# A paged attention cache's rope rows turned by VectorE during the projection, kept in DRAM, and read back as keys

## What is computed

```python
def step(carry, pages):                  # one page of 128 rows per sequence
    m, l, acc = carry
    ck = cache_ckv[pages]                # (8, 128, 256) latent rows
    kr = cache_krope[pages]              # (8, 128, 64)  rotary key rows
    s = mla_scores(q_lat, q_rope, ck, kr)    # q_lat.ck + q_rope.kr, scaled
    m_new = jnp.maximum(m, jnp.max(s, axis=-1))
    alpha = jnp.exp(m - m_new)
    p = jnp.exp(s - m_new[..., None])
    l = l * alpha + jnp.sum(p, axis=-1)
    acc = acc * alpha[..., None] + jnp.einsum('bhqk,bkc->bhqc', p, ck)
    return (m_new, l, acc), None
(m, l, acc), _ = lax.scan(step, (m0, l0, acc0), page_table.T)
```

## Time and profile before

| what | value |
|---|---|
| median of three runs | 2065.1 us (2063.27 to 2066.8) |
| the profiled execution's own time | 2068.19 us |
| its span, first to last instruction | 2066.4 us |
| TensorE busy | 1892.8 us (92%) |
| VectorE, ScalarE, GpSimd busy | 594.6, 443.1, 274.8 us |
| mean granted TensorE clock | 0.953 of full speed |
| moved by DMA | 400.28 MB, mean 194 GB/s |

### The profile page before, as it was taken

How to read it: one execution, slowest core, us unless ns; L and a number is a source line. 1 busy time by engine, 2 the same in 40 slices (tenths; PEclk the granted TensorE clock), 3 DMA queues, 4 the chain that set the end, 5 groups by cost and what they waited for, 6 DMA issues and landing times. The chain is left out here.

```text
span 2066.4 us, 27202 instructions
## 1 busy us (share of the span) xinstructions
PE 1892.8 (92%) x10878; PEld 1122.3 (54%) x10878; DVE 594.6 (29%) x1362; ACT 443.1 (21%) x934; POOL 274.8 (13%) x420
## 2 busy tenths in 40 slices
PE   7999999999999999988999997999498888988884
PEld 5644444444445656755666664565365555555551
DVE  3110000000003334334555555566412211111116
ACT  3211111100013333222444443222111101111103
POOL 1021111000000000002222220122411211111100
PEclk9999999999999999998999998999699899999997
DMA  8212220222110000005777775435589999999986
GB/s 250 82 72 73 78 73 31 78 78 78 58 53 1 1 1 1 1 0 224 286 269 280 274 271 217 178 131 181 197 347 420 420 418 412 418 403 402 409 334 253
DMA packets 91425, 400.28 MB, mean 194 GB/s; under 512 B 22656, under 2 KB 28256, under 8 KB 60544
## 3 DMA queue, kind: packets, MB, share of 16 engines
q1 hardware_dynamic: 71040, 297.50, 36.9%
q0 software_dynamic: 20160, 101.24, 13.0%
q10 hardware_dynamic: 128, 0.20, 0.0%
HBM read 372.44 MB, written 46.88 MB: 203 GB/s over the span
## 5 line engine op out<-in xcount | busy, mean ns | idle before, releaser
L795 PE MATMUL psum<-arena 128*128 128x512 f32 (+1 forms) x1280 | 526.1, 566 | 0.0
L795 PEld LDWEIGHTS psum<-arena 128*128 128x128 f32 x1280 | 238.9, 189 | 259.2 <-issue 234.7
L1224 PE MATMUL psum<-arena 128*64 128x256 f32 (+1 forms) x2048 | 286.4, 414 | 66.2 <-DMA arena<-in_w_up_dram 65.7
L1224 PEld LDWEIGHTS psum<-arena 128*64 128x64 f32 (+1 forms) x2048 | 204.8, 156 | 137.9 <-issue 82.2
L1839 DVE COPY arena<-psum 128x512 f32<-128x512 f32 (+5 forms) x52 | 27.8, 545 | 522.2 <-PE psum L863 226.4
L1007 PEld LDWEIGHTS psum<-arena 128*128 128x128 f32 x1280 | 142.2, 142 | 29.3 <-issue 26.0
L1007 PE MATMUL psum<-arena 128*128 128x128 f32 x1280 | 153.8, 276 | 2.4 <-DVEq L1887 2.4
L1243 PE MATMUL psum<-arena 128*64 128x512 f32 (+1 forms) x512 | 131.3, 595 | 0.7 <-DVE arena L2153 0.7
L1393 ACT ACTIVATE arena<-psum 128x512 f32<-128x512 f32 (+1 forms) x72 | 40.5, 562 | 411.8 <-PE psum L795 401.0
L1410 ACT COPY arena<-psum 128x512 f32<-128x512 f32 x160 | 90.5, 587 | 176.5 <-PE psum L1007 176.5
L1895 DVE COPY arena<-psum 128x512 f32<-128x512 f32 x160 | 109.8, 692 | 36.3 <-PE psum L1007 33.7
(11 more groups left out here) (304 smaller groups left out, 1941.2 us busy)
## 6 DMA issues: line engine op xcount, KB each, us to landing
arena<-in_w_gate_dram SPq DMA_DIRECT2D x64, 1024.0 KB, 12.0
arena<-in_w_up_dram SPq DMA_DIRECT2D x64, 1024.0 KB, 20.6
arena<-in_w_down_dram SPq DMA_DIRECT2D x64, 1024.0 KB, 22.0
arena<-in_w_in_dram SPq DMA_DIRECT2D x8, 2048.0 KB, 7.9
z_act<-arena SPq DMA_DIRECT2D x64, 256.0 KB
arena<-z_act SPq DMA_DIRECT2D x8, 2048.0 KB, 10.4
arena<-in_x_prompt_dram SPq DMA_DIRECT2D x16, 512.0 KB, 4.8
arena<-y_rows SPq DMA_DIRECT2D x8, 1024.0 KB, 9.9
```

The costliest lines, as they stand in the source:

```text
L795: last = mm(out[:, 0:w], xn_t[:, k, t * P:t * P + P], w_blk[n % 2][:, k, 0:w], start=(k == 0), stop=(k == KD - 1))
L1224: last = mm(bank(2 + u)[rows, DE * x:DE * x + DE], xg_t[u][:, k, rows], w_e[slot][x][:, k, :], start=(k == 0), stop=(k == KD - 1))
```

## The change

The rope rows leave stage 3's gather and its transposes.

In stage 1, once the early units are done, GpSimd gathers the `kr` rows of all 32 chunks one after the other into two raw buffers, VectorE turns each in two instructions of 32x32 blocks (128 x 512 each) into two turned buffers, and SyncE stores them with two transfers a chunk to a new DRAM scratch `rope_t` of 64 features by 2048 keys a chunk (16.8 MB in all). The stores stand in SyncE's list behind the z stores of tiles 42 to 57, two chunks a tile. GpSimd reaches its barrier only when all are stored.

In stage 3 SyncE loads one chunk's turned rows, 64 partitions of 8 KB, into one of four places (two tiles, upper or lower 64 partitions), from three scores ahead. A chunk is now eight units on four banks, and the rope round of `score` reads its keys from that place in pieces of 32 columns, all four products on the same half of the partitions. The other edits are bookkeeping: key rows of a unit are consecutive, one semaphore carries two former ones, and the counts of waits follow.

```diff
+FIRST_ROPE = 42
...
+        pre = [attn_base + 5 * D]
+        kr_raw = [take(PG * DR, pre).rearrange("p (r n) -> p r n", r=PG) for _ in range(2)]
+        kr_b = [take(PG * DR, pre).rearrange("p (c m) -> p c m", c=2) for _ in range(2)]
+        rope_t = nc.dram_tensor("rope_turned", [NCH * DR, PG * P], F32, kind="Internal").ap()
...
-        kr = [take(PG * DR, o).rearrange("p (r n) -> p r n", r=PG) for _ in range(4)]
+        kr_t2 = [take(PG * P, o) for _ in range(2)]
-        kr_tt = take(2 * 512, o).rearrange("p (g n) -> p g n", g=2)
...
-        turn_units = [("c", 0, 0), ("c", 0, 1), ("r", 0, 0), ("c", 1, 0), ("c", 1, 1),
-                      ("c", 2, 0), ("c", 2, 1), ("r", 1, 0), ("c", 3, 0), ("c", 3, 1)]
+        turn_units = [(j, c) for j in range(4) for c in range(2)]
...
+        def rope_home(n):
+            return kr_t2[n % 4 // 2][DR * (n % 2):DR * (n % 2) + DR, :]
+        PRE = NCH // 2
...
+            def rope_store(n):
+                sp.wait_ge(rk_t, n + 1)
+                for c in range(2):
+                    rows = DR * n + 32 * c
+                    sp.dma_start(rope_t[rows:rows + 32, :].rearrange("f (a m) -> a f m", a=4),
+                                 kr_b[n % 2][:, c, :]).then_inc(rk_mv[n % 2], 16)
...
+                    for n in range(2):
+                        if FIRST_ROPE <= b * NT + t < FIRST_ROPE + NCH // 2:
+                            rope_store(2 * (b * NT + t - FIRST_ROPE) + n)
...
+            def rope_load(n):
+                if n >= 4:
+                    sp.wait_ge(c_s, n - 3)
+                sp.wait_ge(rk_mv[n % 2], 32 * PRE + 16 * (n // 2))
+                sp.dma_start(rope_home(n), rope_t[DR * n:DR * n + DR, :]).then_inc(rk_mv[n % 2], 16)
...
             sp.wait_ge(ends, 8)
+            for n in range(2):
+                rope_load(n)
...
+            for n in range(2, NCH):
+                rope_load(n)
...
-                    if u >= 5:
-                        pe.wait_ge(kt_in[(u - 5) % 2], 5 * n + (u - 5) // 2 + 1)
+                    if u >= 4:
+                        pe.wait_ge(kt_in[u % 2], 4 * n + (u - 4) // 2 + 1)
...
+                rope = rope_home(q).rearrange("p (a r k) -> p r a k", a=4, r=PG)
...
-                                  ck_t[:, c, j, :] if c < 2 else kr_tt[half, j // 2, :], start=(c == 0), stop=(c == 2))
+                                  ck_t[:, c, j, :] if c < 2 else rope[:, 4 * j:4 * j + 4], start=(c == 0), stop=(c == 2))
...
-                        turned(n + 1, (6, 8))
+                        turned(n + 1, (6,))
...
+            for n in range(NCH):
+                if n >= 2:
+                    pool.wait_ge(rk_t, n - 1)
+                off = bass.IndirectOffsetOnAxis(ap=page_int[:, n:n + 1].bitcast(U32), axis=0)
+                pool.indirect_dma_start(kr_raw[n % 2].rearrange("p r c -> p (r c)"), None, kr_g, off).then_inc(c_in[n % 2], 16)
+            for u in range(2):
+                pool.wait_ge(rk_mv[u], 32 * PRE)
             stage_end(pool, 1)
...
-                pool.indirect_dma_start(kr[q].rearrange("p r c -> p (r c)"), None, kr_g, off).then_inc(c_in[q], 16)
...
+            for n in range(NCH):
+                dve.wait_ge(c_in[n % 2], 16 * (n // 2 + 1))
+                if n >= 2:
+                    dve.wait_ge(rk_mv[n % 2], 32 * (n // 2))
+                for c in range(2):
+                    last = V.transpose(kr_b[n % 2][:, c, :].rearrange("p (r k) -> p r k", r=PG),
+                                       kr_raw[n % 2][:, :, 32 * c:32 * c + 32])
+                last.then_inc(rk_t, 1)
             stage_end(dve, 1)
```

More of the change, by code:

```diff
@@ L440, in build @@
         z_stored = [sem(f"z_stored{i}") for i in range(2)]
-        lat_stored = sem("latent_stored")
+        rows_stored = sem("cache_rows_stored")
         lat_ready = sem("latent_ready")
@@ L456, in build @@
         c_tr = sem("cache_turned")
+        rk_t, rk_mv = sem("rope_blocks_turned"), [sem(f"rope_rows_moved{i}") for i in range(2)]
         kt_in = [sem("turned_by_act"), sem("turned_by_dve")]
@@ L506, in build @@
         block = ctx.enter_context(nc.Block())
[L510 to L511 removed]
+        turn_units = [(j, c) for j in range(4) for c in range(2)]
         NU = len(turn_units)
         def key_row(j, kk):
[L516 removed]
+            return 4 * j + kk
         def turned_at(u):
[L519 to L520 removed]
+            j, c = turn_units[u]
+            return ck_t[:, c, j, :]
+        def rope_home(n):
+            return kr_t2[n % 4 // 2][DR * (n % 2):DR * (n % 2) + DR, :]
+        PRE = NCH // 2
         def group_moves(what, n, out):
@@ L691, in _ @@
             sp.wait_ge(y_mm, NT)
-            sp.wait_ge(v_st, 16)
+            sp.wait_ge(rows_stored, 80)
             w_load(3, 3)
@@ L996, in turn, with score @@
                 for u in us:
-                    if u >= 5:
-                        pe.wait_ge(kt_in[(u - 5) % 2], 5 * n + (u - 5) // 2 + 1)
+                    if u >= 4:
+                        pe.wait_ge(kt_in[u % 2], 4 * n + (u - 4) // 2 + 1)
                     elif not first:
-                        pe.wait_ge(kt_in[(u + 5) % 2], 5 * n - 5 + (u + 5) // 2 + 1)
-                    kind, j, c = turn_units[u]
+                        pe.wait_ge(kt_in[u % 2], 4 * n - 4 + (u + 4) // 2 + 1)
+                    j, c = turn_units[u]
                     for kk in range(4):
[L1003 to L1007, removed]
+                        last = tr(bank(u % 4)[:, P * kk:P * kk + P], ck[q][:, key_row(j, kk), P * c:P * c + P], ident)
                     last.then_inc(c_tr, 1)
-            def score(n):
+            def score(n, q, loads):
+                half = slice(DR * (q % 2), DR * (q % 2) + DR)
+                rope = rope_home(q).rearrange("p (a r k) -> p r a k", a=4, r=PG)
                 for e in range(2):
-                    pe.wait_ge(kt_in[e], 5 * n + 5)
+                    pe.wait_ge(kt_in[e], 4 * n + 4)
+                pe.wait_ge(rk_mv[q % 2], 32 * PRE + 16 * loads)
                 for c in range(3):
                     for j in range(4):
-                        half = slice(DR * (j % 2), DR * (j % 2) + DR)
                         last = mm(bank(5)[RS * j:RS * j + RS, :], q_now[:, c, :] if c < 2 else qr_now[half, :],
-                                  ck_t[:, c, j, :] if c < 2 else kr_tt[half, j // 2, :], start=(c == 0), stop=(c == 2))
+                                  ck_t[:, c, j, :] if c < 2 else rope[:, 4 * j:4 * j + 4], start=(c == 0), stop=(c == 2))
                 last.then_inc(c_s, 1)
@@ L1034, in weigh @@
                 last.then_inc(c_pv, 1)
-            pe.wait_ge(c_in[0], 32)
+            pe.wait_ge(c_in[0], 16 * PRE + 16)
             turn(0, 0, range(NU), first=True)
             pe.wait_ge(q_ready, 1)
-            score(0)
+            score(0, 0, 1)
             def batch(i, last_batch):
@@ L1054, in batch @@
                             pe.wait_ge(q_ready, i + 2)
-                        score(n + 1)
+                        score(n + 1, (q + 1) % 4, 2 * i + (q + 1) // 2 + 1)
             with pe.Fori(0, NB - 1) as i:
@@ L1409, in turned @@
                     act.wait_ge(c_tr, NU * n + u + 1)
-                    nc.scalar.copy(turned_at(u), bank(u % 5)).then_inc(kt_in[0], 1)
+                    nc.scalar.copy(turned_at(u), bank(u % 4)).then_inc(kt_in[0], 1)
             act.wait_ge(n_dve, 3)
@@ L1603, in _ @@
                     G.tensor_tensor(v[1][0:r, :, 32:64], tmp[0:r, 2], tmp[0:r, 3], ALU.add).then_inc(qrope_done, 1)
+            kr_g = cache_krope[0].rearrange("n (a r) c -> (n a) (r c)", r=PG)
+            pool.wait_ge(idx_ready, 1)
+            pool.wait_ge(b_mm[0], groups_done(sched, ("G1", NTP))[0])
+            pool.wait_ge(b_mm[1], groups_done(sched, ("sR", 0))[1])
+            for n in range(NCH):
[5 more added lines that the diff above has]
+                pool.wait_ge(rk_mv[u], 32 * PRE)
             stage_end(pool, 1)
@@ L1870, in _ @@
             copy(qr_now, qsr[:, 0:RS]).then_inc(q_ready, 1)
-            dve.wait_ge(lat_stored, 64)
+            dve.wait_ge(rows_stored, 64)
             V.memset(acc, 0.0)
@@ L1894, in turned @@
                     dve.wait_ge(c_tr, NU * n + u + 1)
-                    copy(turned_at(u), bank(u % 5)).then_inc(kt_in[1], 1)
+                    copy(turned_at(u), bank(u % 4)).then_inc(kt_in[1], 1)
             turned(0, range(1, NU, 2))
```

17 lines of the change are left out of this document (8 added, 9 removed).

## The result

The changed kernel is slower: 2145.33 us, median of 4 runs (2136.13 to 2149.79), beside 2064.44 before (4 runs, 2063.27 to 2066.8); ratio 1.0396, 95% interval 1.0373 to 1.0419. Its profiled execution took 2136.13 us, with a span of 2134.3. The forecast was 2043, in a range of 2035 to 2062.

The account below looks back on a forecast made before the run. TensorE was taken to bound the projection and cache stages, DMA weight streaming the expert stage. 2068.2 - 28.4 (cache) + 6 (projection) = 2045.8; as the runs' median is 3.1 lower, forecast 2043 us, range 2035 to 2062.

Parts of the forecast that it names:

- A store of 512 KB lands after 4.0 us: Projection: time for a rope store to land, 4.0 us taken from rows showing 4.0 and 5.9.
- One pair, alone: Projection: two chunks' stores and transposes fit in a 6.88 us z tile, with 1.3 us to spare.
- I take the growth of the delay per full tile as 0: Projection: SyncE falls no further behind in full tiles, though traffic takes 5.8 to 6.7 us of 6.88.
- 6 lost at growth 0: Projection: short tiles and W_in loads make SyncE 21 us late, 15 are absorbed, 6 us lost.
- Rival (b): Projection: turning slower than tiles from tile 44, each us per pair 14 us of waiting, 2075; chance 0.10, half of it 0.09.
- The wait of weigh: Cache stage: ScalarE's probability copy ends before TensorE reaches weigh, 0.13 us to spare; price 0, at most 0.2 a chunk.
- Strided read: Cache stage: the rope round reading keys in runs of 32 columns costs 0; at half rate 0.94 a chunk, 30 us.
- unit 5: Cache stage, four banks: VectorE's copy of unit 1 ends at 1105.29, before TensorE needs it at 1105.58; no cost.
- The rope load: Cache stage: load to 64 partitions takes at most 2.8 us, transfers 8.3 us a chunk, under the 8.6 period; time unchanged.
- The coupling by SyncE's list: Projection: rope stores share SyncE's list with z stores, for which ScalarE and then TensorE wait; 6 us lost.
- VectorE's late start: Cache stage: once in four chunks VectorE starts about 2.0 us into the turn; 0.15 us wait, seven times, +1.0.
- rival (c): Cache loop: strided read or wait of weigh gives back 6 to 30 us, 2049 to 2067; chance 0.08 together with another rival.

Follow-up runs that it names:

- e2: Changed kernel with one unused row behind each 32 scratch rows, so the store destination stays [4][32][512] but its pieces are contiguous: 2147.49 us, one execution.
- e3: Changed kernel with store destination one [128][512] block, scratch rows 2048 wide, so 2 KB pieces keep the 8 KB pitch: 2063.25 us, one execution.
- e7: Changed kernel with store destination [2][64][512] instead of four outermost entries, and four load transfers a chunk: 2305.91 us, one execution.
- e1: Changed kernel with each store's destination one contiguous [128][512] block, and two load transfers a chunk: 2060.73 us (10 runs), ratio 0.999 to the kernel before.
- e6: Changed kernel with [128][512] stores, two chunks a tile, and three raw and three turned buffers instead of two each: 2037.04 us, one execution.
- e10: The three-buffer kernel with [128][512] stores and two chunks a tile, unchanged and timed again: 2033.78 us (4 runs), ratio 0.986 to the kernel before.
- e5: Changed kernel with [128][512] stores and one chunk a z tile, tiles 39 to 70: 2047.59 us (6 runs), ratio 0.9921 to the kernel before.
- e9: Kernel with [128][512] stores and one chunk a tile, started at tile 38 instead of 39: 2037.54 us (6 runs), ratio 0.9884 to the kernel before.
- e8: Kernel with one chunk a tile and the change's own stores, each rope load issued twice in a row: 2153.91 us, one execution.

## Why the prediction was wrong

**The step that failed** is "A store of 512 KB lands after 4.0 us", in "One pair, alone", and with it "I take the growth of the delay per full tile as 0". The store of the earlier trace rows from which 4.0 came writes 128 rows in one block and so runs on all engines. The rope store writes four blocks of 32 rows. At most 102 GB/s are left for it, against 410 in the earlier trace rows; in the kernel after, store n was issued from 514.56 on and its buffer came free for the transposes of chunk n+2 at 527.07: 12.5 us in place of 4.0. A pair took 13.4 us, 6.5 more than a tile. The prediction had the row's bytes right and overlooked the shape.

What the runs show is e2, e3 and e7: the time goes with the number of blocks at the outermost level (2, 4, 128), not with the pitch or the length of the pieces. The Trainium skill (DMA: Bandwidth & Descriptors, Why a DMA increments its semaphore by 16 and not by 1) states the rule: the number of engines is the largest one up to 16 that divides the slowest dimension of both access patterns. By that 4 and 128 give 4, 2 and 128 give 2, 128 and 128 give 16; the plateaus at 2 and 1 tenths, 102 and 51 GB/s, agree. The prediction draws on the Trainium skill for the load's partitions and the transposes and not for the store's shape, where this rule spoke against the change.

**The right sum, by the prediction's own terms:** 6 lost at growth 0, and 14 full tiles x 6.5 = 91, make 97 of the 106.8 measured; the 10 left over are not assigned (the clock is one candidate). The same sum gives 240 for the 270 that e7 lost (16.7 more than a tile), and 20 for the 19 of e1 (7.9 us a pair, from 51.3 us for 13 chunks, 466.61 to 517.92 in its timeline). Rival (b) named this mechanism, with its wait, its queue and "each us per pair is 14 us of waiting". What the prediction named as the sign of (b), a projection over 28 us longer, is what came. But the upper end of (b) was 2.3 us, from transposes of 1.23, and its landing of 5.9 us came from another store of one block. With 13.4 it gives 2068.2 - 28.4 + 97 = 2137, and the profiled execution took 2136.13; that they agree so closely is luck, as the 10 us missing in the projection and 2 in the cache stage stand against 12 us by which the three other stages came out shorter in this execution. So the range was too narrow on one term: no row showed a store with an outermost dimension of four, and its bound should have been a quarter of the rate.

**A second term was left out:** the gather in the series of two buffers. The first one in the kernel after, before any rope store, shows its length (the second gather is issued 1.5 us behind it, so it is not quite alone). Timeline, GpSimd's issue:

```profile
383.30 1.16 POOL L1639 DMA_INDIRECT arena<-in_cache_krope_dram,arena  x1 [3.77 <-PE psum L966]
```

and VectorE's transposes behind it:

```profile
387.69 1.31 DVE L1897 STREAM_TRANSPOSE arena<-arena 128x512 f32<-128x512 f32 x2 [4.46 <-DMA arena<-in_cache_krope_dram,arena]
```

4.4 us, and 1.3 for the transposes that must end before the buffer is gathered again: 5.7 us for one buffer's round, and so for a pair on two buffers, with little beside it; that leaves 1.2 us of a tile for all that traffic adds. In e1, with stores on all engines, this series is what keeps a pair at 7.4 to 8.9 us, and the loss is 19 us and not 6. Three buffers (e6, e10), or half the pace (e5, e9), take it away.

**What was right.** Two units of 0.46 us gone from each chunk. The wait of weigh: the prediction had 0.13 us of cover; there is a wait of 0.17 for ScalarE's copy on the row, and a chunk takes 8.68 where 8.61 was forecast, some 2 us in the stage. Cache stage -26.6 us for -28.4. Strided read 0, unit 5 without a wait, transposes 0.65 us. The rope load: forecast at most 2.8 us and a chunk of transfers at most 8.3; the kernel after has 1.9 and 8.8, e8 2.3 and 8.2, so the load was bounded rightly and the sum was not, and TensorE didn't wait for it all the same. The cover is thin: the share of the DMA engines from 1110 to 1200 is 1.01, while TensorE is busy 90.00 of 90. The Trainium skill (SBUF — State Buffer, Door 1: The DMA port swizzle) measures 196 GB/s for 1 MiB to 64 partitions, in the prediction an estimate of 2.7 us for the load; the 1.9 and 2.3 lie between that and the 1.4 by bytes. The time won before the expert stage is kept for the most part: e9's cache stage is 28.4 us shorter in the profiled execution, and its median lies 22.5 us below that of before; the 6 between are not assigned. The coupling by SyncE's list, z stores to ScalarE to TensorE, is the one forecast; only its size was not.

**Two slips in the prediction's numbers** change nothing. By its own rows VectorE's late start is 1114.50 - 1112.89 = 1.6 us into the turn and not 2.0; the 0.15 us priced for it go with 1.6. And 30 us back from the forecast in rival (c) end at 2073, not 2067.

## What to carry to other kernels

Before a store or load is priced by another one's row, compare the outermost dimensions of both access patterns, not only bytes and KB: four blocks at that level ran here at a quarter of the rate, and the cure was a layout in which the 128 rows are one dimension, with no byte less. When background transfers share a queue with stores that the bound engine waits for, write out the whole loop (gather, turning, store, for each buffer) beside the period that it must fit in; if it is near, one more buffer or half the pace in twice the tiles gives the slack, and the last transfer must land before the next barrier.

## What the runs showed of the hardware

- A DMA from 128 partitions to four blocks of 32 rows of 2 KB ran at 102 GB/s and to two blocks of 64 at 51, 25.5 GB/s an engine if four and two engines carry them; the same rows as one block at a pitch of 8 KB cost about what contiguous ones do (2063.25 us in one execution, 2058.37 to 2064.89 in ten).
- TensorE's granted clock fell within the projection when its products came in pieces with waits between, to 0.76 from 460 to 520 and 0.64 in e7's same stretch, which showed 1.00 in e9 at the same place. These are mixtures of two levels: in the kernel after the clock was 0.50 (1.2 GHz) from 507 to 511, behind a wait of 4.07 us, and in e7 0.50 from 614.6 to 620, behind one of 20.10, and 1.00 (2.4 GHz) from 620.5 to 624. So products behind such a stall took longer too: 615 us for the 583 of the stage before.
- A transfer on few engines showed in the DMA view as a plateau, 102 GB/s at 2 tenths and 51 GB/s at 1 tenth, beside long waits for that transfer.
- A product whose moving operand is read in runs of 32 columns went as fast as one read in a row (2.84 and 2.83 us for the score).
- TensorE can stay fully busy (90.00 of 90 us) at a DMA share of 1.01: the share alone doesn't say that transfers bind. A gather's packets made 6.8 us of engine time there and 5.9 in e8.
